# Expert products of 512 columns, split operands at equal addresses modulo 512, and modulation steps of the first stage moved

## What is computed

```python
def modulation(c, w, b):
    return jnp.split(jax.nn.silu(c) @ w + b, 3, axis=-1)      # shift, scale, gate

def sandwich(x, mod, g_pre, g_post, fn):
    shift, scale, gate = mod
    h = rms_norm(x, g_pre) * (1.0 + scale[:, None]) + shift[:, None]
    return x + gate[:, None] * rms_norm(fn(h), g_post)

# hier_moe: 16 experts in 4 groups, width 256 each; a token takes one group and two experts in it
hid = jax.nn.silu(jnp.einsum('td,edf->tef', t, w_gate)) * jnp.einsum('td,edf->tef', t, w_up)
hid = hid * combine.astype(hid.dtype)[:, :, None]
out = jnp.einsum('tef,efd->td', hid, w_down)
```

## Time and profile before

| | |
|---|---|
| median of 3 runs | 1543.95 us |
| the profiled execution | 1546.48 us |
| its span | 1544.6 us |
| TensorE, VectorE, ScalarE busy | 94%, 75%, 53% |
| HBM read | 331 MB, 215 GB/s over the span |

### The profile page before, as it was taken

One profiled execution on the slowest core, in us unless ns is written; L12 is line 12 of the kernel. 1 busy time (PEld: TensorE's weight loads), 2 busy tenths in 40 slices (PEclk: granted clock), 3 DMA queues, 4 the chain that ended last, 5 costly groups with the idle time before them and its releaser, 6 DMA issues.

```text
span 1544.6 us, 25597 instructions
## 1 busy us (share of the span) xinstructions
PE 1459.0 (94%) x10156; PEld 1336.0 (86%) x10156; DVE 1153.7 (75%) x1737; ACT 812.9 (53%) x1177; POOL 1.2 (0%) x5
## 2 busy tenths in 40 slices
PE   7988999999999999999999799999989999999996
PEld 7877799999998979999978678899979987898995
DVE  4887876875856656697478977889969754888995
ACT  1431433434443345535575437887745554677773
POOL 0000000000000000000000000000000000000000
PEclk8889999999999999999999999999999999999998
DMA  9882689986565515565633135999924542689990
GB/s 376 297 301 71 218 300 323 339 289 205 192 204 165 164 42 178 176 190 179 188 104 122 69 125 207 357 343 379 333 66 139 165 136 69 211 333 350 340 368 34
DMA packets 184202, 333.94 MB, mean 216 GB/s; under 512 B 13308, under 2 KB 127508, under 8 KB 184084
## 3 DMA queue, kind: packets, MB, share of 16 engines
q1 hardware_dynamic: 184084, 332.31, 63.0%
HBM read 331.18 MB, written 1.09 MB: 215 GB/s over the span
## 4 chain that ended last, share of the span: by engine, by line
PE 75%; DVE 11%; ACT 3%; issue 3%; DMA 1%; ACTq 0%; DVEq 0%
PE PSA L604 15%; PE PSA L606 15%; PE PSA L605 15%; PE PSA L601 9%; PE PSB L604 6%; PE PSB L606 6%; PE PSB L605 6%; PE PSB L601 2%; DVE WL L1804 2%; DVE T L1804 2%; ACT WH L1327 1%; DMA WR<-ffn_w_in 1%; DVE AR L1804 1%; DVE ACC L1801 1%; ACT T L1317 1%
## 5 line engine op out<-in xcount | busy, mean ns | idle before, releaser
L1804 DVE TENSOR_TENSOR WL<-WR,WH 128x1024 fp32r<-128x1024 f32 x352 | 421.3, 1219 | 134.7 <-ACT WH L1327 134.3
L1327 ACT CAST WH<-WR 128x1024 fp32r<-128x1024 f32 x352 | 354.9, 1048 | 109.5 <-DMA WR<-hyb_w_in 42.5
L604 PE MATMUL PSA<-XH,WH 128*128 128x256 f32 x1312 | 378.0, 288 | 6.8 <-DVE AR L2188 2.5
L606 PE MATMUL PSA<-XH,WL 128*128 128x256 f32 x1312 | 373.2, 284 | 0.0
L605 PE MATMUL PSA<-XL,WH 128*128 128x256 f32 x1312 | 372.6, 284 | 0.0
L604 PEld LDWEIGHTS PSA<-XH,WH 128*128 128x128 f32 x1312 | 250.6, 191 | 11.1 <-issue 2.8
L605 PEld LDWEIGHTS PSA<-XL,WH 128*128 128x128 f32 x1312 | 251.0, 191 | 1.1 <-issue 0.5
L606 PEld LDWEIGHTS PSA<-XH,WL 128*128 128x128 f32 x1312 | 249.8, 190 | 0.0
L1804 DVE TENSOR_TENSOR WL<-AR,WH 128x1024 fp32r<-128x1024 f32 x152 | 178.3, 1219 | 22.1 <-ACT WH L1327 22.1
L604 PE MATMUL PSB<-WH,GH 128*128 128x512 f32 x448 | 179.7, 401 | 3.0 <-DVE GL L1804 3.0
L606 PE MATMUL PSB<-WH,GL 128*128 128x512 f32 x448 | 177.6, 396 | 0.0
(11 more groups left out here) (260 smaller groups left out, 2250.4 us busy)
## 6 DMA issues: line engine op xcount, KB each, us to landing
WR<-ffn_w_in SPq DMA_DIRECT2D x88, 512.0 KB, 4.6
AR<-ada_w SPq DMA_DIRECT2D x58, 512.0 KB, 8.2
AR<-moe_w_down SPq DMA_DIRECT2D x56, 512.0 KB, 6.4
AR<-moe_w_gate SPq DMA_DIRECT2D x48, 512.0 KB, 6.1
AR<-moe_w_up SPq DMA_DIRECT2D x48, 512.0 KB, 6.2
WR<-ffn_w_out SPq DMA_DIRECT2D x44, 512.0 KB, 4.6
WR<-att_w_qkv SPq DMA_DIRECT2D x36, 512.0 KB, 5.0
AD<-ada_w SPq DMA_DIRECT2D x34, 512.0 KB, 5.8
```

What stands on the lines that cost most here:

```text
L604: e.matmul(o, lh, rh, start=start, stop=False, skip_group_check=True)
L606: return e.matmul(o, ll, rh, start=False, stop=stop, skip_group_check=True)
L1327: A(e.copy(hi_slot(m), raw_slot(m)), s_hi)
L1804: return e.tensor_tensor(o, i, j, op)
```

## The change

Three things are done at once.

1. Gate and up weights of an expert are put side by side in memory (1024 x 512), and a piece holds 2 rows per partition of 512 columns instead of 4 of 256. `gate_and_up` makes 24 matmuls of 512 columns for a job.
2. `MC`, `SM`, `CT` and `PR` are allocated last. All tiles of split operands then start at 128 modulo 512 bytes.
3. In the first stage, parts 3 and 4 of the modulation change places (gate rows of block 0, then shift of block 1), the steps stand at other pieces, two more places in `AR` take loads, and the gate rows' sum goes to banks 4 and 5. They are read by VectorE after the last level (`ada_end(3)`), with four steps behind (`ADA_BEHIND_LEVELS`). TensorE waits for that read before `down(0, ...)`.

TensorE, in a job of the first MoE: before, around the two transposes and from there to the down pieces (61 matmuls of the program from one pair of transposes to the next).

The gate rows and four steps stand ahead of the conversion there. The diff, cut:

```diff
@@ -121,9 +121,8 @@
             if i < NJOB * 4:
-                for half in range(2):
-                    out.append(("moe_w_gate_2", "m", (l, i // 4, i % 4), 0, half))
-                    out.append(("moe_w_up_2", "m", (l, i // 4, i % 4), 0, half))
+                for part in range(4):
+                    out.append(("moe_w_gate_up", "m", (l, i // 4, i % 4), 0, part))
             if i:
@@ -142,8 +141,11 @@
 STAGES = list(FIRST)
-ADA_PARTS = [(0, 1), (0, 0), (1, 1), (1, 0), (0, 2), (2, 1), (2, 0), (1, 2), (3, 1), (3, 0), (2, 2), (3, 2)]
+ADA_PARTS = [(0, 1), (0, 0), (1, 1), (0, 2), (1, 0), (2, 1), (2, 0), (1, 2), (3, 1), (3, 0), (2, 2), (3, 2)]
 ROWS_LOADED = 12
+ADA_BEHIND_LEVELS = (32, 33, 34, 35)
@@ -151,20 +153,22 @@
     at = 1
-    for p, rate in ((2, 1), (3, 2), (4, 2), (5, 1), (6, 1), (7, 1), (8, 1), (9, 1), (10, 1), (11, 1)):
+    for p in range(2, 12):
         n, part = ADA_PARTS[p]
...
             at = FIRST["att"] + 2
-        offsets = (0, 1, 2, 2, 3, 3, 4, 4) if p == 3 else [k // rate for k in range(8)]
+        pieces = {3: (12, 12, 13, 13, 16, 17, 17, 18), 4: (22, 22, 22, 22, 23, 24, 25, 26)}.get(p, range(at, at + 8))
         for k in range(8):
-            step.setdefault(at + offsets[k], []).append(8 * p + k)
-        last = at + offsets[7]
-        if part == 2:
+            if 8 * p + k not in ADA_BEHIND_LEVELS:
+                step.setdefault(pieces[k], []).append(8 * p + k)
+        last = pieces[7]
+        if part == 2 and p != 3:
             last = max(last, FIRST[STAGES[n]] + ROWS_LOADED + 8)
         total[last + 1] = p
-        end[last + (3 if p < 5 else 4)] = p
+        if p != 3:
+            end[last + (3 if p < 5 else 4)] = p
         at = last + (4 if p < 5 else 5)
@@ -187,6 +191,7 @@
     piece = {x: n for n, xs in ADA_STEP.items() for x in xs}
+    piece.update((x, 22) for x in ADA_BEHIND_LEVELS)
     place, count, before, load = [], [], [], {}
@@ -194,8 +199,10 @@
             i = (0, 1, 11, 12, 17, 16, 15, 11)[x - 16]
+        elif x < 32:
+            i = (0, 1, 16, 15, 18, 19, 20, 21)[x % 8]
         elif x < 40:
-            i = (0, 1, 16, 15, 18, 19, 20, 21)[x % 8]
+            i = (0, 1, 18, 28, 29, 19, 20, 21)[x % 8]
         elif x < 80:
@@ -205,8 +212,8 @@
         if x >= 20:
-            early = piece[x] - (9 if 24 <= x < 28 else 3 if 28 <= x < 32 else 6)
-            if i >= 22:
+            early = piece[x] - (9 if 24 <= x < 28 else 3 if 28 <= x < 32 else 8 if 32 <= x < 40 else 6)
+            if 22 <= i < 28:
                 early = max(early, FIRST["ffn", 0])
@@ -373,22 +380,22 @@
         RS = sb("RS", 1024)
-        MC = sb("MC", 168)
-        SM = sb("SM", 800)
-        CT = sb("CT", CN)
-        PR = sb("PR", PN)
         WR = sb("WR", NRAW * 1024)
...
         AR = sb("AR", ARENA)
+        MC = sb("MC", 168)
+        SM = sb("SM", 800)
+        CT = sb("CT", CN)
+        PR = sb("PR", PN)
         scratch = nc.dram_tensor("bias_rows", [24, 384], F32, kind="Internal")
...
         s_raw = [sig(f"s_raw{i}_landed") for i in range(NRAW + NFAR)]
-        s_ada = [sig(f"s_ada{i}_landed") for i in range(28)]
+        s_ada = [sig(f"s_ada{i}_landed") for i in range(30)]
         s_hi, s_lo, s_used = sig("s_hi_made"), sig("s_lo_made"), sig("s_piece_used")
@@ -397,6 +404,11 @@
         pring = Ring(6, [sig(f"s_bank{i}_filled").sem for i in (6, 7)], [sig(f"s_bank{i}_free").sem for i in (6, 7)])
+        gring = Ring(4, [sig(f"s_bank{i}_filled").sem for i in (4, 5)], [sig(f"s_bank{i}_free").sem for i in (4, 5)])
+        def ada_ring(p):
+            return pring if p < 2 else gring if p == 3 else ring
@@ -480,6 +492,7 @@
         ada_at += [AR[:, x:x + 1024] for x in range(7168, 13312, 1024)]
+        ada_at += [AR[:, x:x + 1024] for x in (0, 5376)]
         accs = (ACC[:, :], AR[:, 1024:2048])
@@ -623,7 +636,7 @@
                 acc = accs[p == 1]
-                u = use(("ada", p), 2 if part == 2 else 1, of=pring if p == 0 else ring)
+                u = use(("ada", p), 2 if part == 2 else 1, of=ada_ring(p))
                 e.wait_ge(s_adastep.sem, ada_count(8 * p + 7))
@@ -872,6 +885,7 @@
             t.then_inc(u.fill[0], 1)
+            e.wait_ge(*gring.uses["ada", 3].free)
             down(0, 1, True, False)
@@ -1134,23 +1148,22 @@
-                def gate_or_up(u, i, up, half):
+                def gate_and_up(u, i, part):
                     n, h, lo = piece()
-                    h, lo = v3(h, 4), v3(lo, 4)
+                    h, lo = v3(h, 2), v3(lo, 2)
                     j = i // 4
...
                         jh, jl = (x[:, :, tile * P:tile * P + P] for x in (xh, xl))
-                        if i % 4 == 0 and not up:
-                            e.wait_ge(s_xlj.sem, 4 * l + 2 * tile + half + 1)
+                        if i % 4 == 0 and part % 2 == 0:
+                            e.wait_ge(s_xlj.sem, 4 * l + 2 * tile + part // 2 + 1)
                     else:
                         jh, jl = emix[(j - 1) % 2]
-                        if i % 4 == 0 and not up:
+                        if i % 4 == part == 0:
                             e.wait_ge(s_mix.sem, 2 * (NJOB - 2) * l + 2 * j)
-                    for k in range(4):
-                        kk = 4 * half + k
-                        t = mm3(bank(u.b, up * 256, up * 256 + 256), jh[:, kk, :], jl[:, kk, :], h[:, k, :],
-                                lo[:, k, :], up == kk == 0, kk == 7)
+                    for k in range(2):
+                        kk = 2 * part + k
+                        t = mm3(bank(u.b), jh[:, kk, :], jl[:, kk, :], h[:, k, :], lo[:, k, :], kk == 0, kk == 7)
                     t.then_inc(used(n)[0], 1)
@@ -1198,13 +1211,12 @@
                         u.piece = taken[0] + 3
-                        gate_or_up(u, i, 0, 0)
+                        gate_and_up(u, i, 0)
                     if i:
...
                     if i < NTURN:
-                        gate_or_up(u, i, 1, 0)
-                        gate_or_up(u, i, 0, 1)
-                        gate_or_up(u, i, 1, 1)
+                        for part in range(1, 4):
+                            gate_and_up(u, i, part)
                     if i == 0:
@@ -1845,12 +1857,13 @@
                 n, part = ADA_PARTS[p]
-                u = (pring if p < 2 else ring).uses["ada", p]
+                u = ada_ring(p).uses["ada", p]
                 filled(u)
...
                     V.wait()
-                    V.frees(tt(RS[:, :], PSA[:, u.b * 512:u.b * 512 + 1024], RS[:, :], ALU.add), u)
+                    ps, o = (PSA if u.b < 4 else PSB), u.b % 4 * 512
+                    V.frees(tt(RS[:, :], ps[:, o:o + 1024], RS[:, :], ALU.add), u)
                     V.wait()
@@ -2120,6 +2133,9 @@
                         V.frees(e.copy_predicated(dst, rep(mask, 4), v3(bank(u.b), 4)), u)
+            ada_end(3)
+            for x in ADA_BEHIND_LEVELS:
+                ada_step(x)
             ss, o = ring.uses["ss"], ring.uses["o"]
@@ -2722,8 +2738,10 @@
                     e.wait_ge(s_adastep.sem, ada_count(ADA_BEFORE[x]))
-                elif 18 <= i < 22:
+                elif 18 <= i < 22 or i == 28:
                     e.wait_ge(s_dif.sem, 1)
+                elif i == 29:
+                    e.wait_ge(s_gh.sem, 1)
                 elif i >= 22:
@@ -2901,6 +2919,7 @@
         arrays[n] = np.ascontiguousarray(f[n])
+    arrays["moe_w_gate_up"] = np.concatenate([f["moe_w_gate_2"], f["moe_w_up_2"]], 3)
     qkv = f["att_w_qkv"].copy()
...
         heads = qkv[..., c:c + 512].reshape(-1, 4, 2, 64)
```

More of the change, by code:

```diff
@@ L2845 @@
         "even_w_in_2", "s5_w_glu_2", "even_w_out_2", "odd_w_in_2", "odd_w_out_2",
-        "moe_w_gate_2", "moe_w_up_2", "moe_w_down_2"]
+        "moe_w_down_2"]
 def kernel(**inputs):
```

## The result

The changed kernel takes 1528.52 us (median of 4 runs, 1526.88 to 1529.14); the kernel before 1546.02 (4 runs, 1541.48 to 1553.11). The ratio is 0.9877, 95% interval 0.9848 to 0.9906: 1.2% faster, 17.5 us in medians, where 1505.7 us and 38 us had been forecast, and 0.5 us above the end of the forecast range. The profiled executions differ by 18.2 us in span, 1544.6 against 1526.4.

The account below looks back on a forecast made before the run. TensorE was taken as the bound. Experts 8, FFNs 14.9, mixers 8.6 and first stage 2 + 4.7 summed to 38.2 us: 1508.3 from the profiled 1546.5, or 1505.7 against the median; range 1490 to 1528.

Parts of the forecast that it names:

- The bound: Whole kernel: TensorE, busy 94% of the span, bounds it; matmul spacing counts fully in FFNs, mostly in mixers, conditionally in experts.
- Wide products: 512-column matmuls: equal addresses modulo 512 bytes bring spacing from 234 to 227 ns, 7.4 ns each.
- rival B: Wide-product spacing: the 8 ns come from the tile, not the address; 1537 us, chance 0.09.
- Experts: Expert jobs: wide products and equal addresses save 12.6 us at TensorE, 8 kept, bounds 2 and 12.6; jobs 8.4 us.
- rival C: Experts: held by VectorE or the DMAs (375 GB/s a share of 1), no gain there; 1514 us, chance 0.1.
- Narrow products: 256-column matmuls outside the experts: equal addresses save 5.2 ns each, bounded at 0 and 13; spacing 113 to 116.
- two interpolations: Narrow-product saving: half the wide saving by columns, 3.7 ns, or one bubble in 17, 6.7 ns; 5.2 taken between.
- wide products elsewhere: 512-column matmuls outside the experts: 864 at 7.4 ns each, 6.4 us before the shares kept in mixers and first stage.
- rival D: Narrow products: equal addresses delay weight loads, 8 ns more on 4608 products; slower, 1562 us, chance 0.03.
- Rival A: All matmuls: alignment counts for wide products only; 19 us gained, 1525 us, chance 0.16.
- First stage: Before the first FFN: moved modulation steps save 4.7 us net, bounds 2 and 8; alignment another 2 kept of 3.2.
- the new wait: First stage, fourth level: TensorE, ready at 102.5, gets its factors near 106, a wait of 3.6 us.

Follow-up runs that it names:

- v3b: Same kernel as v3, timed again: changed kernel with XH at +128 and XL at +224 modulo 256 by tile order; 1518.30 us, ratio 0.9818 to the kernel before.
- the old places: Changed kernel with MC, SM, CT and PR allocated ahead of WR again, wide expert products and moved steps kept; 1540.92 us, ratio 0.9963 to the kernel before.
- half-width run: Changed kernel with each 256-column product in the first FFN made as two of 128, each with its own weight load; that FFN became 159 us longer.
- the sweeps: Changed kernel with its tiles in other orders, here and there padded, to vary start addresses; the first two took 1526.5 and 1533.9 us in one execution each.
- v3: Changed kernel with only the tile order changed, XH at +128 and XL at +224 modulo 256 from the weights; 1519.3 us in one execution.

## Why the prediction was right in sign and wrong in size

- **The bound.** Right where it was tried: what TensorE's spacings gave, the time gave. The jobs, 0.29 us shorter, gave 9.3 us in the experts (40 x 0.29 = 11.6, of which longer pauses took some back), and v3b's 2.9 ns on 3936 narrow products (11.4 us, less 1.4 in the experts) moved the time by 8 to 11 us.
- **Wide products.** Right in mechanism, a little over in size: 7.4 ns forecast, 234.2 to 227.7 = 6.5 measured. The 7.4 is what a product gains in a long run of them (234.2 to 226.7); the first ten behind each break gain less. The earlier trace rows could not show it, since its row begins behind the first of them. Addresses, not tiles, make it (rival B is out): `T2R` against `ARR` went from 235 to 227 and in the old places back to 235. The Trainium skill, "SBUF — State Buffer", section "Who interferes with whom", has TensorE's two read ports independent of each other, by which places would make no difference. The runs (234.1 and 227.7) do not agree, though they do not show that the ports are the cause. The modulus was wrong: it is 256.
- **Experts.** 8 us forecast, 9.3 measured, with jobs of 8.43 us (8.4). VectorE has 98.47 us in the 107.1 us window, as before, and TensorE's cover did get thin: a job with a pause behind it is 9.95 us against 8.43, 1.52 more, before 10.07 against 8.72, 1.35 more. The DMA engines moved 398 GB/s in the stretch that had 388, so rival C's ceiling at 375 is no ceiling.
- **Narrow products: the step that failed.** The trace had no aligned one, and the estimate bounded the gain at 0 and 13 ns and took 5.2 from between, by two interpolations that both let the narrow product be a shorter wide one. It was 0.0 with `XH` moving (120.2, 119.4, 120.2 to 119.9) and a loss of 1.7 where weights move (118.1 to 119.8). The prediction's own sign of being wrong, that narrow spacings stay, is what came. These terms carried 11.0 in the FFNs, 7.3 in the mixers and 1.6 in the first stage: 19.9 of 38.2 us. What is left, 18.3, is what the spans show, 18.2, but that it fits to 0.1 is luck: the experts gave 9.3 for 8, the first stage 5.3 for 4.7, and wide products elsewhere 3.6 for 5.6. The prediction named its own counter-evidence under rival D, that a narrow product needs nearly all of its time for the weight load, and then used 107 as its floor. The half-width run puts the floor at 111.6, which leaves 8 ns to gain and not 13, and the sweeps show that equal places are not where they are gained: 119.9 there, 117.0 in v3.
- **Rival A** (wide ones alone, 1525 us, given 0.16) is what happened. It had "half or more of the excess" against it, which counted the columns at full rate as the floor, the same mistake.
- **First stage.** 4.7 for the moved steps, by rows 5.3, alone 4.9 in the median of ten runs (by the interval 1.4 to 7.7). In single traces the granted clock moves the end of this stage by as much as the steps do. The last level product, the new wait and the late half of the output features came within 0.6 us of the forecast. The 2 us for alignment there did not come apart from this; 1.6 of them were narrow ones.
- **Range.** It reached over A at 1525 by 3 us; A had 6.4 for wide products outside the experts, and 3.6 came for all that is left. The reference moved as well: the kernel before had a median of 1546.0 in 4 runs, 1543.95 in the 3 on which the forecast stood.

## What to carry to other kernels

Before a rate seen on one shape is carried to another, ask what bounds the other shape: a run of the same product at half its width shows it at once (111.7 where the 256-column spacing read as columns and a fixed rest would give 67). A layout change can need its partner: equal places gave nothing to narrow expert products, width gave next to nothing at unequal places, both together gave 8 to 10 us more than the two alone. Where matmuls follow each other without a gap, the places of stationary and moving tiles modulo 256 bytes are worth a short sweep, since they cost nothing but the order of allocation.

## What the runs showed of the hardware

- Products of 512 columns with rounded operands: 227.7 ns in the mean with both operands at equal places modulo 256 bytes (227 to 230 by kind, 226.7 once ten or so have followed each other), 229 to 236 elsewhere. Of 256 columns: 115.5 to 122.1, by the places of more than the two operands, 119.9 at equal ones. Of 128, measured at equal places only: 111.6. Plain float32 products of one column, each with its load of 128x128: 112. Behind a wait or a pair of transposes up to ten or so wide products at equal places are slower, mostly 227 to 236 each (in the kernel before, in put_back, only three); at the old places they are at 233 to 236 like the rest.
- TensorE without a pause is no guarantee of its clock. In the half-width run, in the FFN whose narrow products move 128 columns per load, it was busy 40.00 of 40 us in each of two windows, with 1.00 granted in one and 0.67 in the other, which is 1.2 GHz in place of 2.4 for two thirds of it. The same spacing then is 213 or 214 instead of 111.6 ns, and the 512-column ones in between are 430 instead of 227.
- In the first stage after, 3.08 us of waiting at a granted clock of 0.99 were followed by 16 products at 0.51 (3.63 against 1.95 us), which is 1.2 GHz in place of 2.4. The wait of 1.07 us before it was followed by none: the granted clock stayed at 1.00.
